# One decoder layer on one core: GLA gate products, stores of the conv tails, and waits for halves

## The reference

```python
h = rmsnorm(x, g_mix);  proj = h @ w_in          # GLA q|k|v|r|code, GDN qkv, z, a, b
gate_pre = code @ gla_w_gate2 + gla_b_gate       # rank 16
la = log_sigmoid(gate_pre) / 16                  # GLA decay per key channel
conv = silu(causal_conv4(qkv));  new_buf = last 3 rows of the conv's input
g = -exp(a_log) * softplus(a + dt_bias);  beta = sigmoid(b)
o_a, s_gla = gla_chunked(q, k, v, la, s_gla)     # prompt; a recurrent step for samples
o_b, s_gdn = gdn_chunked(q, k, v, g, beta, s_gdn)
x = x + concat(norm(o_a)*silu(r), norm(o_b)*silu(z)) @ w_out
x = x + cross_attention(rmsnorm(x), mem_k, mem_v)
h = rmsnorm(x, g_ffn)
x = x + (silu(h @ w_gate) * (h @ w_up)) @ w_down # D 2048, D_FF 5632
```

## Time and profile before

| | us |
|---|---|
| median of 3 runs (lowest, highest) | 1935.27 (1934.59, 1937.45) |
| the profiled execution | 1934.49 |
| its span | 1932.8 |
| PE busy (share of the span) | 1840.9 (95%) |
| PE weight load busy | 1736.6 (90%) |
| DVE busy | 1148.1 (59%) |
| ACT busy | 762.3 (39%) |
| POOL busy | 207.5 (11%) |
| share of PE in the chain that ended last | 88% |

### The profile page before, as it was taken

How to read it: one execution, slowest core, us unless ns; L and a number is a source line. 1 busy time by engine, 2 the same in 40 slices (tenths; PEclk the granted TensorE clock), 3 DMA queues, 4 the chain that set the end, 5 groups by cost and what they waited for, 6 DMA issues and landing times.

```text
span 1932.8 us, 34051 instructions
## 1 busy us (share of the span) xinstructions
PE 1840.9 (95%) x13801; PEld 1736.6 (90%) x13801; DVE 1148.1 (59%) x1584; ACT 762.3 (39%) x765; POOL 207.5 (11%) x205
## 2 busy tenths in 40 slices
PE   5999989988999899999999999999999999999996
PEld 3999979986999899888647999999999999999996
DVE  5788437742777657655456656665444566665443
ACT  1554525423353253334442344443333344433333
POOL 7000000001014500000002520000000000000331
PEclk9999989998999999999999999999999999999998
DMA  5655525435215657777784578888455888985552
GB/s 163 207 176 179 179 91 175 140 118 151 88 56 178 192 177 246 269 272 255 274 272 128 174 196 242 252 247 231 138 179 179 226 237 243 250 229 152 171 181 81
DMA packets 413949, 367.01 MB, mean 190 GB/s; under 512 B 11375, under 2 KB 373870, under 8 KB 412806
## 3 DMA queue, kind: packets, MB, share of 16 engines
q1 hardware_dynamic: 386486, 340.85, 57.4%
q10 hardware_dynamic: 27392, 25.17, 4.0%
HBM read 347.84 MB, written 18.35 MB: 189 GB/s over the span
## 4 chain that ended last, share of the span: by engine, by line
PE 88%; DVE 6%; ACT 2%; issue 2%; DMA 1%; POOL 1%; SPq 1%; DVEq 0%; POOLq 0%; ACTq 0%
PE ps L450 63%; PE ps L525 9%; PE ps L506 4%; DVE w_lo L431 2%; PE ps L1358 2%; PE ps L931 1%; PE ps L492 1%; PE ps L1170 1%; ACT w_hi L424 1%; PE ps L1366 1%; PE ps L1088 1%; PE ps L1185 1%; PE ps L1018 1%; PE ps L1327 1%; PE ps L1096 1%
## 5 line engine op out<-in xcount | busy, mean ns | idle before, releaser
L424 ACT ACTIVATE w_hi<-raw 128x2048 fp32r<-128x2048 f32 (+1 forms) x285 | 512.2, 1797 | 945.8 <-PE ps L450 769.0
L431 DVE TENSOR_TENSOR w_lo<-raw,w_hi 128x2048 fp32r<-128x2048 f32 (+1 forms) x285 | 619.4, 2174 | 299.8 <-ACT w_hi L424 296.6
L450 PE MATMUL ps<-act_hi,w_lo 128*128 128x264 f32 x2576 | 741.0, 288 | 11.8 <-DVE w_lo L431 8.8
L450 PE MATMUL ps<-act_lo,w_hi 128*128 128x264 f32 x2576 | 733.0, 285 | 0.0
L450 PE MATMUL ps<-act_hi,w_hi 128*128 128x264 f32 x2576 | 732.4, 284 | 0.0
L450 PEld LDWEIGHTS ps<-act_hi,w_lo 128*128 128x128 f32 x2576 | 488.6, 190 | 16.4 <-issue 9.5
L450 PEld LDWEIGHTS ps<-act_lo,w_hi 128*128 128x128 f32 x2576 | 489.0, 190 | 0.4
L450 PEld LDWEIGHTS ps<-act_hi,w_hi 128*128 128x128 f32 x2576 | 486.1, 189 | 0.0
L450 PE MATMUL ps<-ff_hi,w_lo 128*128 128x264 f32 x704 | 201.9, 287 | 4.3 <-DVE ff_lo L641 4.3
L450 PE MATMUL ps<-ff_hi,w_hi 128*128 128x264 f32 x704 | 201.4, 286 | 0.0
L450 PE MATMUL ps<-ff_lo,w_hi 128*128 128x264 f32 x704 | 200.9, 285 | 0.0
(11 more groups left out here) (404 smaller groups left out, 2115.9 us busy)
## 6 DMA issues: line engine op xcount, KB each, us to landing
raw<-in_w_in_dram SPq DMA_DIRECT2D x56, 1024.0 KB, 7.0
raw<-in_ffn_w_gate_dram SPq DMA_DIRECT2D x44, 1024.0 KB, 5.9
raw<-in_ffn_w_up_dram SPq DMA_DIRECT2D x44, 1024.0 KB, 10.3
raw<-in_ffn_w_down_dram SPq DMA_DIRECT2D x32, 768.0 KB, 4.8
raw<-in_ffn_w_down_dram SPq DMA_DIRECT2D x32, 640.0 KB, 6.1
raw<-in_w_out_dram SPq DMA_DIRECT2D x16, 1024.0 KB, 6.6
raw<-in_xa_w_q_dram SPq DMA_DIRECT2D x16, 1024.0 KB, 6.9
raw<-in_xa_w_k_dram SPq DMA_DIRECT2D x16, 1024.0 KB, 6.8
```

What stands on the lines that cost most here:

```text
L424: act.activation(w_part(ph, w_hi[b]), raw_part(ph, r, half), ACT.Copy)\
L431: dve.tensor_tensor(w_part(ph, w_lo[b]), raw_part(ph, r, half), w_part(ph, w_hi[b]), ALU.subtract)\
L450: mm = pe.matmul(ps[:, acc(ph, u), 0:ph.cols], w[b][:, k, :], v[:, kk + k, 0:ph.cols], start=first and k == 0 and m == 0, stop=last and k ...
```

## The change

Four edits.

1. The gate products go from behind units 1 and 2 to behind units 2 and 4, `gate_logits` from n = 2, 3 to n = 2, 4, ACT's exponentials and logarithms from n = 4, 5 to 5, 6, `decay_rates` and `gate_logs` from n = 6 to 7, and PE's decay products from behind unit 7 into the middle of mixed unit 0.
2. SP issues the nine stores of the tails between the loads of r and those of z, and ACT no longer waits for them.
3. PE waits at dn0 and dn1 for 11 tiles before units 0 and 1 and for all 22 before units 2 and 3; for that the first iteration is written out.
4. `raw_landed` is one semaphore per buffer and part. In gu0, gu1 and mem_v a part is loaded as soon as the unit that used its half is split; in those phases and in mem_k ACT waits only for the part that its half reads.

```diff
-        raw_landed = [sem(f"raw_landed{b}") for b in range(2)]
+        raw_landed = [[sem(f"raw_landed{b}{m}") for m in range(2)] for b in range(2)]
...
-            sp.wait_ge(lo_split, 2 * s + 1)
+            by_half = ph.name in ("gu0", "gu1") or ph.wide and ph.name != "mem_k"
+            sp.wait_ge(lo_split, 2 * s + (0 if by_half else 1))
...
-            for dst, src in parts:
-                sp.dma_start(dst, src).then_inc(raw_landed[r], 16)
+            for m, (dst, src) in enumerate(parts):
+                if by_half and m:
+                    sp.wait_ge(lo_split, 2 * s + 1)
+                sp.dma_start(dst, src).then_inc(raw_landed[r][m], 16)
...
-            act.wait_ge(raw_landed[r], landed)
+            act.wait_ge(raw_landed[r][half], landed)
+            if not (ph.name in ("gu0", "gu1") or ph.wide):
+                act.wait_ge(raw_landed[r][1 - half], landed)
...
             stream("r")
-            stream("z")
-
-            sp.wait_ge(units_done, PH["w_out"].u0 + UNIT_CREDIT)
-            sp.dma_start(gst[:, :, :, :], a["state_gla"][0].rearrange("b h k v -> k b h v")).then_inc(N["sstate_landed"], 16)
-
             W(sp, "tails_copied", 3)
...
+            stream("z")
+
+            sp.wait_ge(units_done, PH["w_out"].u0 + UNIT_CREDIT)
+            sp.dma_start(gst[:, :, :, :], a["state_gla"][0].rearrange("b h k v -> k b h v")).then_inc(N["sstate_landed"], 16)
...
-                if n in (1, 2):
+                if n in (2, 4):
                     pe.wait_ge(scalars_landed, 16 * 3)
-                    W(pe, "scalars", n)
-                    for h in (2 * n - 2, 2 * n - 1):
+                    W(pe, "scalars", n // 2)
+                    for h in (n - 2, n - 1):
...
-                if n == 7:
-                    W(pe, "gdn_g", 1)
...
+            def decay_products():
+
+                W(pe, "gdn_g", 1)
...
             def between(n):
 
+                if n == 0:
+                    decay_products()
...
-                pe.wait_ge(ff_split, HALF_K * (half + 1))
-                phase_pe(pe, PH[f"dn{half}"], ff_hi, ff_lo)
+                ph = PH[f"dn{half}"]
+                pe.wait_ge(ff_split, HALF_K * half + DK_)
+                for u in range(4):
+                    if u == 2:
+                        pe.wait_ge(ff_split, HALF_K * (half + 1))
+                    products(pe, ph, 0, u, ff_hi, ff_lo)
...
-            act.wait_ge(tails_out, 16 * (1 + NB))
...
-                if n in (2, 3):
-                    gate_logits(n - 2)
-                if n == 6:
+                if n in (2, 4):
+                    gate_logits(n // 2 - 1)
+                if n == 7:
                     decay_rates()
                     gate_logs()
-                if n == 7:
                     gate_sums()
```

More of the change, by code:

```diff
@@ L410, in load_part @@
                 sp.wait_ge(lo_split, 2 * s + 1)
-            sp.dma_start(raw[:, r, 8 * m:8 * m + 8, :], kview(wo, 8 * m, 8, 512 + j * 256, 256)).then_inc(raw_landed[r], 16)
+            sp.dma_start(raw[:, r, 8 * m:8 * m + 8, :], kview(wo, 8 * m, 8, 512 + j * 256, 256)).then_inc(raw_landed[r][m], 16)
         def unit_of(ph, i, u):
             s = ph.s0 + u // 2
-            return s % 2, 32 * (s // 2 + i + 1), u % 2, (ph.u0 + u) % 2, ph.u0 + 4 * i + u
+            return s % 2, 16 * (s // 2 + i + 1), u % 2, (ph.u0 + u) % 2, ph.u0 + 4 * i + u
         def split_hi(act, ph, i, u):
             r, landed, half, b, n = unit_of(ph, i, u)
-            act.wait_ge(raw_landed[r], landed)
+            act.wait_ge(raw_landed[r][half], landed)
+            if not (ph.name in ("gu0", "gu1") or ph.wide):
+                act.wait_ge(raw_landed[r][1 - half], landed)
             act.wait_ge(units_done, n + 1)
@@ L461, in half_split_hi @@
             k0 = 8 * (u // 2)
-            act.wait_ge(raw_landed[r], landed)
+            for m in range(2):
+                act.wait_ge(raw_landed[r][m], landed)
             if h:
@@ L986, in gate_prelims @@
                     mm.then_inc(N["turned"], 1)
-                if n == 7:
-                    W(pe, "gdn_g", 1)
-                    for c in range(NC):
-                        pe.matmul(ps[:, 6, c * HB:(c + 1) * HB], tri[:, :], sm(G_)[:, :, c], start=True, stop=True)
-                        mm = pe.matmul(ps[:, 6, (2 + c) * HB:(3 + c) * HB], ones[:, :], sm(G_)[:, :, c], start=True, stop=True)
-                    mm.then_inc(N["gdn_gcol"], 1)
+            def decay_products():
+                W(pe, "gdn_g", 1)
+                for c in range(NC):
+                    pe.matmul(ps[:, 6, c * HB:(c + 1) * HB], tri[:, :], sm(G_)[:, :, c], start=True, stop=True)
+                    mm = pe.matmul(ps[:, 6, (2 + c) * HB:(3 + c) * HB], ones[:, :], sm(G_)[:, :, c], start=True, stop=True)
+                mm.then_inc(N["gdn_gcol"], 1)
             with pe.Fori(0, ph.loops // 2) as i:
@@ L1430, in _ @@
                         products(pe, ph, i, u, act_hi, act_lo)
-                pe.wait_ge(ff_split, HALF_K * (half + 1))
-                phase_pe(pe, PH[f"dn{half}"], ff_hi, ff_lo)
+                ph = PH[f"dn{half}"]
[4 more added lines that the diff above has]
+                    products(pe, ph, 0, u, ff_hi, ff_lo)
+                with pe.Fori(1, ph.loops) as i:
+                    for u in range(4):
+                        products(pe, ph, i, u, ff_hi, ff_lo)
             sum_squares(4, TT)
@@ L1574, in gate_exps @@
             def gate_exps(n):
-                if n == 4:
+                if n == 5:
                     act.wait_ge(scalars_landed, 16 * 3)
@@ L1583, in gate_exps @@
                     act_link(act, act.activation(gaz[:, :, :], gaz[:, :, :], ACT.Exp, scale=-1.0))
-                if n == 5:
+                if n == 6:
                     act.activation(sm(SP_), sm(SP_), ACT.Ln, bias=c1).then_inc(N["scalars"], 1)
```

## The result

| | before | after |
|---|---|---|
| median (lowest, highest), us, 4 runs each | 1936.36 (1934.59, 1937.86) | 1906.07 (1905.87, 1908.21) |
| span of the profiled execution | 1932.8 | 1904.2 |
| PE busy | 1840.9 | 1833.3 |
| mean clock granted | 0.984 | 0.991 |

The ratio is 0.985, with a 95% interval from 0.9836 to 0.9863: faster by 1.5%, 28.6 us between the two spans and 30.3 us between the two medians. It was reached with two of its terms wrong by 1.7 and 1.5 us, in opposite directions.

A forecast was written before the change was run, and what follows sets the result against it. PE, at 95% of the span, was taken as the bound, so only its idle or lower-clock time could be won. Terms -13.6 - 8.0 - 7.9 - 0.4 = -29.9 us gave 1905 us, with bounds 1902.5 to 1909.7 and range 1900 to 1911.

The forecast's parts named there:

- Gate products removed: Units 1 to 3: two waits and two slow units go, the two pairs stay at 2.0 us together; gain 15.6 us.
- The new wait: Middle of mixed unit 0: PE waits 2.0 us for `gdn_g` from `decay_rates`, with no clock lost.
- L1230 row: PE's wait of 2.0 us at that line in the kernel before, which had no slow unit behind it.
- rival (a): Mixed unit 0: the new wait also costs clock, 1.8 us more, 1907 us in all; chance 0.2.
- Rival (b): Mixed unit 0: `gdn_g` comes only with DVE's whole row n = 7, PE stands 7 us; 1912 us; chance 0.04.
- Stores of the tails: `gs1` copy: ACT copies at 430.05 instead of 438.05, PE's wait falls from 11.3 to 3.3 us; gain 8.0 us.
- rival (c): Before L1074: `gst` lands 9 us later and PE waits 2.7 us longer; 1908 us; chance 0.03.
- Down phases: Starts of dn0 and dn1: 2.15 us of wait and 1.78 us of slow unit go at each; gain 7.9 us.
- Rival (d): dn starts: PE waits for a free accumulator instead, so 7.9 us come back; 1913 us; chance 0.03.
- Loads by halves: Start of gu1: the only late load there comes earlier, ACT waiting for the gate part alone; gain 0.4 us.
- Rival (e): Dense stretches, r to gu1: PE is granted less clock, each 1% costing 18.4 us; 1942 us at 2%; chance 0.03.

The follow-up runs named there:

- e6: The changed kernel, not altered, profiled and timed a second time: 1907.09 us, ratio 0.9857 to the kernel before.
- e1: The kernel before with only the gate products, decay products and their helpers moved to later units: 1923.42 us, ratio 0.9941.
- e5: The changed kernel with `decay_rates` behind `gate_logs` in DVE's row n = 7, lengthening PE's new wait: 1909.24 us, ratio 0.9868 to the kernel before.
- e2: The kernel before with only the nine tail stores issued ahead of the z loads and no wait of ACT for them: 1925.72 us, ratio 0.9956.
- e3: The kernel before with only dn0 and dn1 starting on 11 tiles: 1928.01 us, ratio 0.9968.
- e8: The kernel before with only the loads by parts, one semaphore per buffer and part: 1934.53 us, ratio 0.999.

## Why the prediction was right, and where it was not

**Gate products removed: right in kind and nearly in size.** -15.6 forecast, -15.1 at the split of mixed unit 1. Both waits went, and units 1 to 5 ran at 1.00. The term that was mis-sized is the pair of gate products: taken as half of its time at the lower clock, 0.98 us, it costs 7.54 - 6.23 = 1.31 us at full clock. The halving didn't hold: 0.3 us more for the pair measured, and 2.5 us for both (33.67 less five units of 6.23) against the 2.0 taken.

**The new wait: right in place, releaser and length; its clock was mis-sized.** Forecast at 2.0 us, from PE's middle of the unit to DVE's reciprocal behind the split; measured 1.93:

```profile
300.76 0.30 DVE L1988 RECIPROCAL small<-small 128x24 f32<-128x24 f32 x1
```

```profile
301.12 0.39 PE L998 MATMUL ps<-small,tri 128*128 128x8 f32 x2 [1.93 <-DVE small L1988]
```

The clock behind it was taken at 0, since 2.0 us was nearest to the L1230 row, with 1.8 as the bound. It cost 1.7 in after and e6, which the bound covers, and 3.4 in e1, which it doesn't. So rival (a) is what happened at this place, with 0.2 of the chance. The choice of row failed: I chose by the length of the gap alone, and the row with the same length and the same work around it (2.1 us between plain units, at dn) was the better guide. Rival (b), a longer wait, did not come; e5 made it and gives its price.

**Stores of the tails: -8.0 forecast, -8.1 measured for the wait.** The second profile of the kernel before has 12.3 us where the first has 11.3, so a part of this near agreement is chance. The chain of after where the earlier trace rows had SP's 7.70 us and the transfer's 4.94:

```profile
416.64 1.08 ACT gvt L1672 x2
417.73 0.93 ACT gvrow L1674 x2
418.66 0.96 ACT gs L1677 x2
419.62 0.14 issue
419.76 0.46 PE ps L1074 x2
```

PE's wait is 3.15 us, as forecast. The block behind it was taken at 8.3 and took 5.54, 2.8 less, the lower end of the range (5.4). That was luck of the execution in part: over seven profiles with this wait it fell twice, and e2 took 7.17. On the other side L1195 lost 1.6 us in after, with 0.14 chance by the table. Together the stage gave 9.5 us (8.1 + 2.8 - 1.6 = 9.3). `gst` was never next: it landed at 425.0, 14.4 us after its issue, and PE's wait for L1084, 2.99 us as before, ended at 428.29 with DVE's `gsf` (rival (c) is out). The nine stores cost SP less than the 11.0 us that were allowed: 0.35 us for the first instead of 7.70 and 4.06 for the eight others, and z's first load was not late.

**Down phases: -7.9 forecast, -7.84 measured** (3.93 and 3.91), and the same alone in e3. Rival (d) is out. The rule of the Trainium skill ("TensorE: Matmul & The Clock Gate", Why this matters for your kernels), that only gaps of over some 3 us bring the lower clock, would have given 4.3 us. Nine of ten dn starts with a gap of 2.1 us were followed by a fall, and five of seven gaps of 3.15 us were not; the measurement decides against it as a limit. At 1.4 to 1.5 us 42 of 43 gaps had none.

**Loads by halves: -0.4 forecast, -0.48 measured,** in after and alone in e8.

**Rival (e), a lower clock in dense stretches,** did not come: the mean clock rose from 0.984 to 0.991, and the page's slices read 9.

So the sum of -29.9 met 28.8 by the splits, 28.6 by the spans and 30.3 by the medians. The terms: -15.6 became -15.1, +2.0 became +3.7 (1.9 of wait, 1.7 of clock), -8.0 became -9.5, -7.9 became -7.8, -0.4 became -0.5, and 0.3 were lost between the stages. The errors of 1.7 and 1.5 us cancel, and that is luck: each hangs on falls of the clock that the sum didn't price, and e2 and e6 show that they come and go. The range was sound for another reason than the one given: single runs of the changed kernel lie between 1904.5 and 1908.6, somewhat over two falls of the clock apart, and the range covers them.

## What to carry to other kernels

When a wait of TensorE in a dense stretch is priced, look for the row of the same kind of work and the same length. Here waits of 1.9 to 4.0 us among plain units want one slow stretch added (1.7 us, sometimes double; 13 of 14), waits of 1.4 to 1.5 us mostly nothing (42 of 43). When small work is moved to a later unit, check each producer for the queue in front of it: here one helper of 0.94 us, put back one row ahead of a long split where its engine was free, gave 3.5 us on top of the edit. Two profiles of one kernel show some of the stretches at a lower clock that belong to the execution and not to the code; take them before any gain of 2 us is explained. Two are not always enough: both profiles of the kernel before have the fall at dn1 that e8_loads lacks.

## What the hardware showed that was not expected

- The same instructions with the same waits, to 0.01 us, had a fall of the clock behind L1195 in one execution and none in the next (0.66 and 1.00 over 5 us). The eight times of the changed kernel lie in three clusters that far apart: 1904.5; 1905.9 to 1906.3; 1907.9 to 1908.6. That these are falls of the clock is shown for two of them, which have profiles.
- At the decay products the loss was about 1.7 us (0.66 over 5 us) or about twice that (0.50 or 0.55 over 5 us, and 0.92 or 0.77 over the next 5), with nothing between, and it did not grow with the wait: 3.4 behind 1.9 us, and behind 4.0 us 2.9, with the clock down for 1.0 us of the wait too.
- Whether it falls went with length and place together: among plain units 13 of 14 for idle times of 1.9 to 4.0 us and none of 28 for 1.4 and 1.5, in the GDN part 4 of 28 for 2.0 to 2.4. Within one place the cases sort by their moment against the other changes of the clock in the execution. Why was not found.
- A store issued next behind the 4 MB load of `gst` held SP for 7.70 us; the same store ahead of it took 0.35 us, and 0.91 in e2. After the change the store of `gsf` held SP for 7.43 us instead, and nothing waits for it; it is the next issue behind the load of `bst`, 8.9 us after that load's. In nine profiles this store was issued 7.9 to 10.5 us after that load's issue and held SP for 5.8 to 9.4 us, until 16.3 to 17.6 us after it; in the other five it was issued 15.8 to 16.4 us after it and took 0.41 us. So the hold goes with a load still under way; no run took the load away.
